# The four sums of weights of each block of a seven-product matrix multiplication: made by GpSimd in a program of its own, in place of VectorE

## The chip, the cores and the metric

One core of one Trainium2 chip runs the whole program once. The metric is the device time of one execution in microseconds (us). The core has five engines that run their own instruction streams and meet only in semaphores: TensorE (matrix products, into eight PSUM banks), VectorE, ScalarE, GpSimd and SyncE (which here only starts the weight transfers).

## The reference, cut to what matters

Two model blocks run one after the other, all in float32, on 256 tokens (272 from the second block on, with 16 meta tokens in front). The change touches three of the four feed-forward layers of the second block, each with a model width of 1024 and a hidden width of 2816:

```python
def swiglu(x, w_in, w_out):
    g, u = jnp.split(x @ w_in, 2, axis=-1)
    return (jax.nn.silu(g) * u) @ w_out

h = h + 0.5 * swiglu(rms_norm(h, ffn_norm[layer]), ffn_w_in[layer], ffn_w_out[layer])
```

## The kernel before, in words

**Weights.** All large weights come from HBM in one long stream of 128 x 128 tiles, 32 tiles (2 MB) to a chunk. For the second block the chunks go to a ring of six slots in SBUF. SyncE starts a transfer when TensorE has moved on from the chunk that held the slot. The ring is filled from the stream without regard to stages, so at the start of a stage the next chunks may already lie in SBUF.

**Stages.** The program is a row of stages. At the end of each, `end_stage` (L831) makes TensorE, ScalarE and VectorE meet, and GpSimd waits for the same semaphore (L854). In the kernel before GpSimd does nothing in a stage except start the small transfers of constants (`load`, L876).

**The paired stages.** Three stages are `swiglu_pairs` (L2592), called "first", "second" and "third paired stage" below: layer 0's second feed-forward layer, layer 1's first, and layer 1's second, which is the last stage of the program. The first two work on 272 tokens in two halves of 136, the third on 256 in two halves of 128. Each has these parts:

- *Plain columns.* The first 2 x 2 output columns of `w_in` are multiplied as usual (32 products with 272 or 256 tokens, from `xg`). They need only x times the norm's gain, which VectorE writes in eight instructions at the very start (`gained`, L2441 to 2444); the division by the root mean square comes later.
- *Paired columns.* The rest is done by a scheme with seven products in place of eight (Winograd's form of Strassen's): two output tiles x two input tiles x two halves of the tokens. It needs sums of the inputs (`add_inputs`, L2556) and sums of the weights (`add_weights`, L2537).
- *Units.* A unit is one pair of output tiles: 4 groups ("columns" in the code) of seven products for `w_in`, 11 for `w_out`. A stage has 20 units for `w_in` and 4 for `w_out`. Two sets of three PSUM banks take turns, so TensorE may start unit n when VectorE has combined unit n - 2 (`combine`, L2570; `banks_free`).
- *Blocks.* A block is as many groups of four weight tiles as fit in what is left of a chunk: 8 groups when it starts on a chunk's border, fewer at the start and the end of a matrix (`pair_blocks`, L127). The blocks of the first paired stage have 2, 8 (nine times), 6 groups for `w_in` and 2, 8 (five times), 2 for `w_out`; of the second 6, 8 (nine times), 2 and 6, 8 (four times), 6; of the third 4, 8 (nine times), 4 and 4, 8 (five times).
- *Sums of weights.* For a block of n groups four instructions of n x 128 elements are issued: s1 = a21 + a22 (L2548), a21 = a11 - a21 in the ring itself (L2550), s2 = s1 - a11 (L2551), s4 = a12 - s2 (L2553). L2550 waits for L2548, L2553 for L2551. The three results s1, s2, s4 lie in one of two buffers; the sums of block b may be written when TensorE has read the last of block b - 2 (`sums_used`). TensorE multiplies the first two products of a block, which need no sums, and then waits for `sums_ready`.

**The order on VectorE** in a paired stage (L2679 to 2724): gained input (eight instructions), root mean square, normed input (L2686, twice), sums of the inputs (four instructions), sums of weights of the blocks that begin in the first 8 groups, plain columns (L2700 to 2705). Then per pair of units: sums of weights, combine, sums of weights, combine, product of gate and up (L2713), four sums of the hidden values (L2558 to 2563). For the units of `w_out`: sums of weights, combine, new x (L2720), in the first two stages squares (L2724). Before each combine `add_weights` makes the sums of those blocks that begin up to 4 groups behind the unit (L2709, L2717). An instruction of VectorE that waits holds up all behind it.

**ScalarE** copies the first product out of PSUM (L2568), makes silu (L2665), and squares or the output transfers.

Of the kernel before, what the change touches and what calls it, by code (L numbers as in the profile page):

```python
# [15 lines left out]
ALU = mybir.AluOpType  # L16
# [8 lines left out]
DT = D // P  # L25
# [219 lines left out]
class Signal:  # L245
# [3 lines left out]
    def __init__(self, sem, count=0):  # L249
        self.sem, self.posts, self.takes, self.turn, self.turn_post = sem, count, count, None, None  # L250
        self.start = count
# [90 lines left out]
def new_signal(K, name):  # L342

    sem, count = K.spare.pop() if K.spare else (K.new_semaphore(name), 0)
    K.counts.append(Signal(sem, count))
    return K.counts[-1]
# [195 lines left out]
def flat(ap):  # L542
    return ap.rearrange("p a t -> p (a t)")
# [1938 lines left out]
class Sevens:  # L2482
# [5 lines left out]
    def __init__(self, K, st, name, half):  # L2488
        sb = lambda n, shape: st.enter_context(K.nc.sbuf_tensor(name + n, shape, F32))
        self.K, self.half = K, half  # L2490
        self.sums, self.head = sb("_weight_sums", [P, 2, 3, KP * P]), sb("_first_product", [P, 2, half])
        self.sums_ready, self.sums_used, self.first_ready, self.head_ready, self.second_ready, self.third_ready, self.banks_free, self.chain = \
            (new_signal(K, name + n) for n in ("_sums", "_sums_used", "_first_bank", "_first_sb", "_second_bank", "_third_bank", "_banks_free",
                                               "_seven_chain"))
        self.combined = self.banks_free.reader()
        self.blocks, self.block_of, self.units, self.columns, self.summed = [], [], [], 0, 0

# [36 lines left out]
            matmul(K, self.part(n, 2, 0), total(2), x("b22", i), i == 0, last, self.sums_used if o == size - 1 else None, shared=True)  # L2534
            matmul(K, self.part(n, 2, 1), tile(3), x("t4", i), False, last, self.third_ready if last else None, shared=True)

    def add_weights(self, dve, upto):  # L2537

        K = self.K
        while self.summed < len(self.blocks) and self.blocks[self.summed][1] < upto:  # L2540
            b = self.summed
            at, _, size = self.blocks[b]
            if b >= 2:
                dve.wait_ge(*self.sums_used.take())
            dve.wait_ge(*K.weights.loaded_at(at))
            a11, a12, a21, a22 = (K.weights.tiles(at + q * size, size) for q in range(4))
            s1, s2, s4 = (self.sums[:, b % 2, q, 0:size * P] for q in range(3))
            dve.tensor_tensor(out=s1, in0=a21, in1=a22, op=ALU.add).then_inc(*self.chain.post())  # L2548
            dve.wait_ge(*self.chain.posted())
            dve.tensor_tensor(out=a21, in0=a11, in1=a21, op=ALU.subtract)  # L2550
            dve.tensor_tensor(out=s2, in0=s1, in1=a11, op=ALU.subtract).then_inc(*self.chain.post())  # L2551
            dve.wait_ge(*self.chain.posted())
            dve.tensor_tensor(out=s4, in0=a12, in1=s2, op=ALU.subtract).then_inc(*self.sums_ready.post())  # L2553
            self.summed += 1

    def add_inputs(self, dve, b11, b12, b21, b22, t1, t2, t4, last):  # L2556
# [35 lines left out]
def swiglu_pairs(K, gain, layer, last=False):  # L2592

    nc, block, bank = K.nc, K.block, K.bank
# [4 lines left out]
    with ExitStack() as st:  # L2599
# [10 lines left out]
        seven = Sevens(K, st, name, half)  # L2610
# [5 lines left out]
        at = K.weights.at + 2 * PLAIN * DT  # L2616
# [13 lines left out]
        @block.tensor  # L2630
        def _(pe):
            for j in range(PLAIN):
                for f in range(2):
                    for k in range(DT):
                        if j == 0 and f == 0:
                            pe.wait_ge(*rms.hn_ready.take())
                        matmul(K, bank[plain_banks[j][f]][:, 0:T], K.weights.take(pe), xg[:, k, :], k == 0, k == DT - 1,
                               gu_ready if k == DT - 1 else None)
            pe.wait_ge(*x_ready.take())
            for n in range(ins):  # L2640
                if n == 1:
                    pe.wait_ge(*plain_free.take(PLAIN))
                seven.tensor(pe, n, inputs)
            for n in range(ins, ins + outs):
                seven.tensor(pe, n, hidden, h_ready if n == ins else None)
            if not last:
                pe.wait_ge(*sq_added.take(2))
                for q in range(2):
                    nc.tensor.matmul(bank[6][:, 0:T], K.con["ones"][:, :], rms.sq[:, q, :], start=q == 0, stop=False)
                pe.wait_ge(*sq_ready.take(outs))  # L2650
                for q in range(2):
                    ins_ = nc.tensor.matmul(bank[6][:, 0:T], K.con["ones"][:, :], squares[:, q, :], start=False, stop=q == 1)
                ins_.then_inc(*rms.summed.post())
            seven.end(pe)

        @block.scalar
        def _(act):
# [9 lines left out]
            for q in range(outs):  # L2667
# [5 lines left out]
                else:  # L2673
                    if q > 1:
                        act.wait_ge(*sq_added.reader().take(q - 1))
                    act.activation((squares if q else rms.sq)[:, :, :], K.x[:, 2 * q:2 * q + 2, :], ACT.Square).then_inc(*sq_ready.post())

        @block.vector
        def _(dve):  # L2679
            chain = seven.chain  # L2680
            rms.gained(dve, gain, layer, xg, t0)
            rms.inverse_root(dve)
            each = rms.rstd[:, t0:T2].rearrange("p (a t) -> p a t", a=1).to_broadcast([P, DT // 2, T])
            dve.wait_ge(*rms.hn_ready.posted())
            for a in (slice(0, DT // 2), slice(DT // 2, DT)):
                dve.tensor_tensor(out=hn[:, a, :], in0=xg[:, a, :], in1=each, op=ALU.mult).then_inc(*chain.post())  # L2686
            dve.wait_ge(*chain.posted())
            a, b = slice(0, DT // 2), slice(DT // 2, DT)
            seven.add_inputs(dve, hn[:, a, lo], hn[:, a, hi], hn[:, b, lo], hn[:, b, hi], hn_sums[:, 0], hn_sums[:, 1], hn_sums[:, 2], x_ready)
            seven.add_weights(dve, DT)  # L2690

            def turn_over(i):
                dve.wait_ge(*h_mult.posted())
                seven.add_inputs(dve, h[:, 2 * i, lo], h[:, 2 * i, hi], h[:, 2 * i + 1, lo], h[:, 2 * i + 1, hi],
                                 h_sums[:, i, 0, :], h_sums[:, i, 1, :], h_sums[:, i, 2, :], h_ready)

            h_mult = chain
            for j in range(PLAIN):
                dve.wait_ge(*gu_ready.take())
                dve.tensor_tensor(out=s[:, j, :], in0=bank[plain_banks[j][0]][:, 0:T], in1=rms.rstd[:, t0:T2], op=ALU.mult).then_inc(*g_scaled.post())  # L2700
                dve.wait_ge(*gu_ready.take())
                dve.tensor_tensor(out=up[:, j, :], in0=bank[plain_banks[j][1]][:, 0:T], in1=rms.rstd[:, t0:T2], op=ALU.mult).then_inc(*plain_free.post())
            dve.wait_ge(*plain_free.posted())
            dve.wait_ge(*s_ready.take(PLAIN))
            dve.tensor_tensor(out=h[:, 0:PLAIN, :], in0=s[:, :, :], in1=up[:, :, :], op=ALU.mult).then_inc(*chain.post())
            turn_over(0)
            for q in range(0, ins, 2):
                for n, o in ((q, gate), (q + 1, other)):
                    seven.add_weights(dve, seven.units[n][0] + seven.units[n][1] + DT // 2)  # L2709
                    seven.combine(dve, n, o[:, :])  # L2710
                i = (PLAIN + q) // 2
                dve.wait_ge(*silu_ready.take())
                dve.tensor_tensor(out=flat(h[:, 2 * i:2 * i + 2, :]), in0=gate[:, 0:2 * T], in1=other[:, 0:2 * T], op=ALU.mult).then_inc(*chain.post())  # L2713
                turn_over(i)
            for q in range(outs):
                n = ins + q
                seven.add_weights(dve, seven.units[n][0] + seven.units[n][1] + DT // 2)  # L2717
                seven.combine(dve, n, other[:, :])
                new = K.x[:, 2 * q:2 * q + 2, t0:T2]
                dve.scalar_tensor_tensor(out=new, in0=other[:, 0:2 * T].rearrange("p (a t) -> p a t", a=2), scalar=0.5, in1=new, op0=ALU.mult, op1=ALU.add)\  # L2720
                   .then_inc(*y_free.post())
                if not last and 0 < q < outs - 1:
                    dve.wait_ge(*sq_ready.reader().take(q + 1))
                    dve.tensor_tensor(out=rms.sq[:, :, :], in0=rms.sq[:, :, :], in1=squares[:, :, :], op=ALU.add).then_inc(*sq_added.post())  # L2724
# [736 lines left out]
def odd_mixer(K):  # L3461
    nc, block, bank, col = K.nc, K.block, K.bank, K.col
    T = T2
    with ExitStack() as st:
# [80 lines left out]
        def _(dve):  # L3545
# [28 lines left out]


STAGES = [rwkv_branch, hgrn_branch, mlstm_branch, lru_branch, merge_and_router, experts, norm_and_swiglu, even_mixer, lambda K: swiglu_pairs(K, "ffn2_norm_2", 0),
          lambda K: swiglu_pairs(K, "ffn1_norm_2", 1), odd_mixer, lambda K: swiglu_pairs(K, "ffn2_norm_2", 1, last=True)]

# [177 lines left out]
```

## Time and profile before

| | us |
|---|---|
| median of 3 runs (2876.89 to 2882.86) | 2877.27 |
| the profiled execution, by its own time | 2879.56 |
| its span from first to last instruction | 2877.8 |
| TensorE busy | 2781.7 (97%) |
| VectorE busy | 1138.8 (40%) |
| ScalarE busy | 375.3 (13%) |
| GpSimd busy | 28.6 (1%) |

The profile is of one execution. Times are counted from its first instruction. A busy TensorE need not be TensorE at its peak, since products are pipelined and their ends are modelled. The trace records each float32 product as two instructions. "PE" is TensorE's products and "PEld" its weight loads, "DVE" VectorE, "ACT" ScalarE, "POOL" GpSimd; a "q" behind the name is the engine's sequencer. The three paired stages lie at about 2092 to 2315, 2315 to 2537 and 2650 to 2878 us. Spans on GpSimd are rough.

### The profile page before, as it was taken

What the parts mean: (1) busy time and instruction counts of PE and PEld (TensorE: products, weight loads), DVE (VectorE), ACT (ScalarE), POOL (GpSimd) and SP (SyncE); (2) the same over time, 40 slices, a digit from 0 to 9 for tenths busy, and PEclk for the clock granted to TensorE, in tenths of its full rate; (3) what the DMA queues carried; (4) which work ended last, traced back from release to release, by engine and by line L of the source; (5) the groups of instructions that cost most, each with busy time, mean ns of one, the idle gap of its engine ahead of it and who ended that gap; (6) DMA issues with size and microseconds to landing.
All of it is one profiled execution on the core that took longest, in us unless ns stands there. A gap on an engine that the chain in (4) does not pass through costs nothing.

```text
span 2877.8 us, 40524 instructions
## 1 busy us (share of the span) xinstructions
PE 2781.7 (97%) x16939; PEld 1907.5 (66%) x16940; DVE 1138.8 (40%) x2357; ACT 375.3 (13%) x772; POOL 28.6 (1%) x56
## 2 busy tenths in 40 slices
PE   8999999989999999999998999999999999998998
PEld 7977778833333333333335888777799999976998
DVE  2644541222222222222223110462377567546674
ACT  1132420200000000000002000122110010012000
POOL 0000000000000000000000000000000000000000
PEclk9999999999999999999999999999999999999999
DMA  5133244469999999999997433332244444432440
GB/s 210 61 105 117 88 145 164 190 240 425 428 429 428 428 429 427 429 428 429 429 427 298 147 146 140 137 117 88 97 147 154 169 145 148 176 142 73 162 147 16
DMA packets 50080, 655.32 MB, mean 228 GB/s; under 512 B 6016, under 2 KB 8208, under 8 KB 10880
## 3 DMA queue, kind: packets, MB, share of 16 engines
q1 hardware_dynamic: 45696, 642.90, 55.7%
q0 software_dynamic: 3104, 9.48, 1.0%
q8 instruction: 103, 1.69, 0.2%
q10 hardware_dynamic: 1152, 1.05, 0.1%
q14 instruction: 25, 0.20, 0.0%
HBM read 652.36 MB, written 1.05 MB: 227 GB/s over the span
## 4 chain that ended last, share of the span: by engine, by line
PE 81%; DMA 9%; DVE 7%; ACT 1%; issue 1%; PEldq 0%; DVEq 0%; SPq 0%; PEld 0%; ACTq 0%
PE bank L357 70%; DMA weight_ring<-weight_stream 8%; PE bank L1163 2%; PE bank L2169 1%; PE bank L2138 1%; DVE expert_hidden L2271 1%; DVE expert_hidden L2270 1%; PE bank L2160 1%; DVE ffn_weight_sums L2553 0%; DVE ffn_weight_sums L2548 0%; DVE weight_ring L2550 0%; ACT expert_y_slots L2216 0%; DVE ffn_weight_sums L2551 0%; DVE mlstm_qk L1536 0%; DMA first_weight_ring<-weight_stream 0%
## 5 line engine op out<-in xcount | busy, mean ns | idle before, releaser
L357 PE MATMUL bank<-weight_ring,expert_x_slots_t 128*64 128x512 f32 x2048 | 459.2, 599 | 3.9 <-DMA weight_ring<-weight_stream 3.9
L357 PEld LDWEIGHTS bank<-weight_ring,expert_x_slots_t 128*64 128x64 f32 x2048 | 141.1, 137 | 319.1 <-issue 305.0
L357 PE MATMUL bank<-x,first_weight_ring 128*128 128x256 f32 x1376 | 316.3, 385 | 16.3 <-DMA first_weight_ring<-weight_stream 8.7
L357 PEld LDWEIGHTS bank<-x,first_weight_ring 128*128 128x128 f32 x1376 | 260.9, 192 | 59.2 <-issue 18.6
L357 PE MATMUL bank<-ffn_x_normed,weight_ring 128*128 128x136 f32 (+1 forms) x1440 | 243.1, 278 | 0.0
L357 PE MATMUL bank<-weight_ring,expert_hidden_slots_t 128*64 128x512 f32 x1024 | 225.2, 592 | 0.0
L357 PE MATMUL bank<-ffn_h,weight_ring 128*128 128x136 f32 (+2 forms) x1144 | 214.6, 313 | 0.5 <-DVE ffn_up L2788 0.5
L357 PEld LDWEIGHTS bank<-ffn_x_normed,weight_ring 128*128 128x128 f32 x1440 | 201.6, 191 | 0.2
L357 PEld LDWEIGHTS bank<-ffn_h,weight_ring 128*128 128x128 f32 x1144 | 177.6, 190 | 14.7 <-DVE ffn_up L2788 1.0
L2280 DVE TENSOR_TENSOR moe_rows<-moe_rows,bank 128x512 f32<-128x512 f32 x128 | 79.4, 683 | 269.0 <-PE bank L2169 269.0
L357 PEld LDWEIGHTS bank<-weight_ring,expert_hidden_slots_t 128*64 128x64 f32 x1024 | 73.4, 137 | 146.4 <-issue 123.3
L357 PE MATMUL bank<-ffn_x_gained,weight_ring 128*128 128x272 f32 x704 | 162.3, 393 | 1.6 <-ACT ffn_x_gained L2371 1.5
L357 PE MATMUL bank<-ffn_x_sums,ffn_weight_sums 128*128 128x136 f32 (+1 forms) x960 | 149.9, 279 | 8.9 <-DVE ffn_weight_sums L2553 8.9
L357 PE MATMUL bank<-even_hn,weight_ring 128*128 128x272 f32 x624 | 154.7, 403 | 0.0
L357 PEld LDWEIGHTS bank<-ffn_x_gained,weight_ring 128*128 128x128 f32 x704 | 133.0, 190 | 30.4 <-ACT ffn_x_gained L2371 3.1
L357 PEld LDWEIGHTS bank<-even_hn,weight_ring 128*128 128x128 f32 x624 | 118.4, 194 | 28.8 <-issue 2.3
L357 PEld LDWEIGHTS bank<-ffn_x_sums,ffn_weight_sums 128*128 128x128 f32 x960 | 128.1, 191 | 10.5 <-DVE ffn_weight_sums L2553 10.5
L2270 DVE TENSOR_SCALAR expert_hidden<-bank 128x512 f32<-128x512 f32 x32 | 22.1, 692 | 196.4 <-PE bank L357 196.4
L357 PE MATMUL bank<-ffn_h_sums,weight_ring 128*128 128x136 f32 (+3 forms) x456 | 97.2, 329 | 2.1 <-DVE ffn_h_sums L2444 2.1
L357 PE MATMUL bank<-ffn_x_sums,weight_ring 128*128 128x136 f32 (+1 forms) x480 | 94.1, 278 | 0.0
L357 PE MATMUL bank<-ffn_x_normed,ffn_weight_sums 128*128 128x136 f32 (+1 forms) x480 | 94.1, 278 | 0.0
L357 PE MATMUL bank<-ffn_h_sums,ffn_weight_sums 128*128 128x136 f32 (+1 forms) x528 | 82.4, 278 | 3.2 <-DVE ffn_weight_sums L2553 3.2
(659 smaller groups left out, 3179.9 us busy)
## 6 DMA issues: line engine op xcount, KB each, us to landing
weight_ring<-weight_stream SPq DMA_DIRECT2D x276, 2048.0 KB, 15.0
first_weight_ring<-weight_stream SPq DMA_DIRECT2D x29, 2048.0 KB, 7.8
first_weight_ring<-weight_stream SPq DMA_DIRECT2D x4, 512.0 KB, 12.1
x<-x_t SPq DMA_DIRECT2D x2, 512.0 KB, 7.0
out_t<-x ACTq DMA_DIRECT2D x8, 128.0 KB, 2.0
c_ret_ret_q<-const_ret_q POOLq DMA_DIRECT2D x1, 544.0 KB, 5.2
c_ret_ret_k<-const_ret_k POOLq DMA_DIRECT2D x1, 544.0 KB, 6.0
c_odd_pool_inv<-const_pool_inv POOLq DMA_DIRECT2D x1, 544.0 KB, 3.8
```

The source lines that it names most:

```text
L357: ins = K.nc.tensor.matmul(out, lhsT, rhs, start=start, stop=stop, skip_group_check=shared)
L1163: ins = nc.tensor.matmul(out(h), lhsT(h), rhs(h), start=start, stop=stop)
L2138: ins = nc.tensor.matmul(bank[3][rows[g], :], pick[:, b, :], K.x_rows[:, b, g * HW:(g + 1) * HW], start=b == 0, stop=b == 1)
L2160: ins = nc.tensor.transpose(bank[5][:, j * P:(j + 1) * P], h[:, 0, j * P:(j + 1) * P], eye)
L2169: ins = nc.tensor.matmul(bank[4 + 2 * b + g][:, :], spread_t[rows[g], b * P:(b + 1) * P], ys[rows[g], :], start=True, stop=True)
L2270: then(dve.tensor_scalar(h[:, 0, :], bank[1][:, :], 7.0, -7.0, ALU.min, ALU.max))
L2271: dve.scalar_tensor_tensor(out=h[:, 0, :], in0=h[:, 0, :], scalar=1.0, in1=gate[:, 0, :], op0=ALU.add, op1=ALU.mult)\
L2280: ins = dve.tensor_tensor(out=part, in0=part, in1=bank[4 + n][:, :], op=ALU.add)
```

## The change

`add_weights` is issued by GpSimd in a program of its own, for all blocks of the stage one after the other, in place of VectorE, where it stood at three places between other work. It waits for what it waited for before (the block's chunk loaded, the sums of block b - 2 used) and no longer for its place in VectorE's order. Its chain of waits has a semaphore of its own. Buffers, blocks and TensorE's program are unchanged.

```diff
-    def add_weights(self, dve, upto):
+    def add_weights(self, pool, upto):
         K = self.K
         while self.summed < len(self.blocks) and self.blocks[self.summed][1] < upto:
...
             if b >= 2:
-                dve.wait_ge(*self.sums_used.take())
-            dve.wait_ge(*K.weights.loaded_at(at))
+                pool.wait_ge(*self.sums_used.take())
+            pool.wait_ge(*K.weights.loaded_at(at))
...
-            dve.tensor_tensor(out=s1, in0=a21, in1=a22, op=ALU.add).then_inc(*self.chain.post())
-            dve.wait_ge(*self.chain.posted())
-            dve.tensor_tensor(out=a21, in0=a11, in1=a21, op=ALU.subtract)
-            dve.tensor_tensor(out=s2, in0=s1, in1=a11, op=ALU.subtract).then_inc(*self.chain.post())
-            dve.wait_ge(*self.chain.posted())
-            dve.tensor_tensor(out=s4, in0=a12, in1=s2, op=ALU.subtract).then_inc(*self.sums_ready.post())
+            pool.tensor_tensor(out=s1, in0=a21, in1=a22, op=ALU.add).then_inc(*self.sum_chain.post())
+            pool.wait_ge(*self.sum_chain.posted())
+            pool.tensor_tensor(out=a21, in0=a11, in1=a21, op=ALU.subtract)
+            pool.tensor_tensor(out=s2, in0=s1, in1=a11, op=ALU.subtract).then_inc(*self.sum_chain.post())
+            pool.wait_ge(*self.sum_chain.posted())
+            pool.tensor_tensor(out=s4, in0=a12, in1=s2, op=ALU.subtract).then_inc(*self.sums_ready.post())
...
+        @block.gpsimd
+        def _(pool):
+            seven.add_weights(pool, seven.columns)
+
         @block.vector
         def _(dve):
...
-            seven.add_weights(dve, DT)
...
-                    seven.add_weights(dve, seven.units[n][0] + seven.units[n][1] + DT // 2)
                     seven.combine(dve, n, o[:, :])
...
-                seven.add_weights(dve, seven.units[n][0] + seven.units[n][1] + DT // 2)
                 seven.combine(dve, n, other[:, :])
```

## Rows read from the trace of the kernel before

**Rows 1.** The page: busy time by engine, with share and instructions.

```profile
PE 2781.7 (97%) x16939; PEld 1907.5 (66%) x16940; DVE 1138.8 (40%) x2357; ACT 375.3 (13%) x772; POOL 28.6 (1%) x56
```

**Rows 2.** TensorE's waits for VectorE's sums: total us, times, longest, by paired stage in order.

```profile
PEld bank L357 <- DVE ffn_weight_sums L2553: 2.6, 2, 1.3
...
PEld bank L357 <- DVE ffn_weight_sums L2553: 0.2, 1, 0.2
...
PEld bank L357 <- DVE ffn_weight_sums L2553: 11.7, 9, 1.3
```

**Rows 3.** The chain that ended last, third paired stage: start us, us, what.

```profile
2693.35 1.23 DVE ffn_weight_sums L2548
...
2697.00 1.24 DVE ffn_weight_sums L2553
...
2698.28 5.19 PE bank L357 x44
...
2705.45 0.70 DVE ffn_h L2713
...
2707.24 1.23 DVE ffn_weight_sums L2548
```

**Rows 4.** The timeline of ScalarE in the third stage's `w_out`: start, us, engine, line.

```profile
2835.03 0.28 ACT L2568 ACTIVATE ffn_first_product<-bank 128x128 f32<-128x128 f32 x1 [16.92 <-PE bank L357]
...
2852.23 0.28 ACT L2568 ACTIVATE ffn_first_product<-bank 128x128 f32<-128x128 f32 x1 [16.92 <-PE bank L357]
```

**Rows 5.** Groups of VectorE instructions by form: xcount | busy us, mean ns | idle before.

```profile
L2550 DVE TENSOR_TENSOR weight_ring<-weight_ring 128x1024 f32<-128x1024 f32 x41 | 50.2, 1225 | 1.4
L2451 DVE RECIPROCAL x_rms<-x_rms 128x272 f32<-128x272 f32 x3 | 5.6, 1854 | 1.5 <-ACT x_rms L2439 1.5
L2550 DVE TENSOR_TENSOR weight_ring<-weight_ring 128x768 f32<-128x768 f32 x4 | 3.8, 958 | 0.1
L2550 DVE TENSOR_TENSOR weight_ring<-weight_ring 128x512 f32<-128x512 f32 x3 | 2.1, 692 | 0.1
L2550 DVE TENSOR_TENSOR weight_ring<-weight_ring 128x256 f32<-128x256 f32 x4 | 1.7, 426 | 0.1
```

**Rows 6.** The chain again, where the first stage goes from `w_in` to `w_out`.

```profile
2236.57 1.24 DVE ffn_weight_sums L2548
...
2240.22 1.24 DVE ffn_weight_sums L2553
...
2241.50 1.54 PE bank L357 x11
```

**Rows 7.** Windows around the second stage's start; behind the engines' busy times: PEclk, DMA, GB/s.

```profile
2313.00:2315.00 2.00, 1.18 (x4) 0.68 (x4) 0.18 (x1) 0.54 (x2) 0.00 (x0) 0.96 0.82 352
2315.00:2317.00 2.00, 1.76 (x4) 1.41 (x5) 2.00 (x9) 1.04 (x1) 0.00 (x0) 0.50 0.00 0
2317.00:2319.00 2.00, 2.00 (x7) 1.53 (x7) 1.50 (x3) 1.52 (x2) 0.00 (x0) 0.69 0.00 0
2319.00:2321.00 2.00, 2.00 (x11) 1.65 (x10) 1.97 (x2) 0.20 (x1) 0.00 (x0) 1.00 0.00 0
```

**Rows 8.** The timeline of the first stage's start, VectorE and TensorE.

```profile
2091.68 2.26 DVE L2444 TENSOR_SCALAR ffn_h_sums<-x,columns_sb 128x272 f32<-128x272 f32 x8 [1.53 <-PEq L839]
...
2092.10 14.94 PE L357 MATMUL bank<-ffn_h_sums,weight_ring 128*128 128x272 f32 x64 [0.70 <-DVE ffn_h_sums L2444]
...
2096.68 2.49 DVE L2686 TENSOR_TENSOR ffn_x_normed<-ffn_h_sums,x_rms 128x1088 f32<-128x1088 f32 x2
...
2101.36 0.72 DVE L2563 TENSOR_TENSOR ffn_x_sums<-ffn_x_normed,ffn_x_sums 128x544 f32<-128x544 f32 x1
...
2106.87 0.63 PE L357 MATMUL bank<-ffn_x_normed,weight_ring 128*128 128x136 f32 x4
```

**Rows 9.** The timeline of GpSimd and VectorE at the start of another stage.

```profile
2537.97 0.54 POOL L880 DMA_DIRECT2D c_odd_pool_inv<-const_pool_inv  x1
...
2538.40 1.71 DVE L2468 TENSOR_SCALAR odd_y<-x,columns_sb 128x272 f32<-128x272 f32 x6
2538.50 0.64 POOL L880 DMA_DIRECT2D c_odd_pair_gather<-const_pair_gather  x1
...
2540.22 0.54 POOL L880 DMA_DIRECT2D odd_sinks<-in_od_sinks  x1
```

More of the change, by code:

```diff
@@ L2491, in __init__ @@
         self.sums, self.head = sb("_weight_sums", [P, 2, 3, KP * P]), sb("_first_product", [P, 2, half])
-        self.sums_ready, self.sums_used, self.first_ready, self.head_ready, self.second_ready, self.third_ready, self.banks_free, self.chain = \
+        self.sums_ready, self.sums_used, self.first_ready, self.head_ready, self.second_ready, self.third_ready, self.banks_free, self.chain, self.sum_chain = \
             (new_signal(K, name + n) for n in ("_sums", "_sums_used", "_first_bank", "_first_sb", "_second_bank", "_third_bank", "_banks_free",
-                                               "_seven_chain"))
+                                               "_seven_chain", "_sum_chain"))
         self.combined = self.banks_free.reader()
```

## The prediction

> **What bounds the kernel now.** I read the busy line of the page first: TensorE works 97% of the span, VectorE 40%, GpSimd 1% [rows 1]. So only what makes TensorE idle counts, and of that only what VectorE's sums of weights cause. TensorE's waits name them [rows 2]: 2.6 us in the first paired stage (2 waits), 0.2 in the second (1), 11.7 in the third (9). About 14.5 us of 2878 is all that the sums hold up today.
>
> The chain shows how the third stage loses its share [rows 3]. VectorE ends the hidden product and its sums, only then starts the sums of the next block at 2693.35, and TensorE goes on at 2698.28; the next turn begins at 2707.24. A turn of one block of 8 groups (56 products) takes 13.89 us. In the same stage 77 products without a wait take 2852.23 - 2835.03 = 17.20 us [rows 4], so 56 take 12.51. Each turn loses 1.38 us.
>
> **The change, part by part.** The sum is made against the profiled execution, 2879.56 us; the median of the runs is 2.3 us below it, and I move the median by the same difference.
>
> *Removed: VectorE's place in the order.* Of the third stage's nine waits eight are such turns: 8 x 1.38 = 11.0 us. The ninth stands where `w_in` meets `w_out`. Of the first stage's two waits one is of this kind (1.3), the other is at its junction. Gone: 12.3 us, if GpSimd can make a block's sums while TensorE works on one block. VectorE loses some 208 instructions (4 x 52 blocks), about 4.9 us of every 13; it was not the bound, so that alone gives nothing more.
>
> *Price of a sum on GpSimd.* No row shows GpSimd doing arithmetic. The nearest rows are VectorE's: 1.225 us for the same instruction, and at the far end its slowest elementwise one, 1.854 us for 272 elements, which would be 7.0 us for 1024 [rows 5]. The operation is the plain one, so it stands nearer to the first; since both operands must be read I take twice that row: 2.45 us, 9.8 for a block of 8, and by the smaller forms 7.7 for 6 groups, 5.5 for 4, 3.4 for 2. That is below 12.5 to 13.0 us of TensorE per block, so in the steady part the sums are hidden. They stop being so beyond 3.2 us per instruction.
>
> The Trainium skill (GPSIMD Engine Reference, section 3.1) gives 4497 ns for 2048 float32 elements on GpSimd and 2293 on VectorE. From that I estimate 2.28 us for 1024. By that price the junctions below would cost 2 us less. No run here shows it yet; VectorE's 1.225 us agrees with it.
>
> *Added: the junctions.* The sums of block b start when block b - 2 is used up, that is when TensorE starts b - 1. If b - 1 is small and b large, nothing covers them. In the first stage block b - 1 has 2 groups: 14 products and the two that need no sums last 3.7 us (16 products of 136 tokens, at between 17.20/77 = 0.223 us, the third stage's with 128 tokens, and 136/128 of that, 0.237). VectorE needed 4.93 us (2236.57 to 2241.50 [rows 6]) and TensorE idled 1.2 to 1.3. GpSimd at 9.8 leaves 6.1. In the second stage 6 groups follow 2: 7.7 - 3.7 = 4.0, against 0.2 today. In the third 8 groups follow 4: 9.8 - 6.7 = 3.1, against 1.2. Added: 13.2 - 2.7 = 10.5 us.
>
> *Clock.* An idle TensorE can lose clock: after the pauses at the end of the first stage its granted clock stood at 0.50, the level of 1.2 GHz, for 2 us and at 0.69 for 2 more [rows 7]. That is 2 x 0.5 + 2 x 0.31 = 1.6 us lost. I count one such loss, at the 6 us pause; bounds 0 and 4.8.
>
> So far: -12.3 + 10.5 + 1.6 = -0.2 us. The large expected gain is eaten by three junctions.
>
> *Moved: the sums of the first two blocks to the stage's very start.* Before, VectorE made them after the inputs, under the plain products. GpSimd starts them with the stage, since b below 2 waits for nothing but the chunk, and the ring is full (no transfer runs in 2315 to 2321 [rows 7]). In just these microseconds VectorE has its only work that TensorE waits for at once: eight gained inputs in 2.26 us, the first of which lets TensorE start 0.4 us later; products last 14.94/32 = 0.467 us, so the eighth input is wanted about 3.7 us into the stage [rows 8]. Whether an instruction of VectorE is delayed by one of GpSimd that reads the same memory, no row shows. The lower bound is no delay. The upper bound is turn by turn: each input behind the first waits out one GpSimd instruction. I take a middle: GpSimd pauses twice in a block for its own chain, and VectorE gets two through in each pause, so that the eight wait out the four sums of block 0 and one of block 1. First stage (2 groups): 3.4 + 2.45 + 2.2 of its own = 8.1, wanted at 3.7: +4.4. Second (6): 7.7 + 2.45 + 2.2 = 12.3: +8.6. Third (4): 5.5 + 2.45 + 2.1 = 10.1, wanted at 3.5: +6.6. Together +20 us. Turn by turn with three large sums in place of one adds 4.9 to each: +34. Behind them, normed inputs and their sums end at 2102.1 where TensorE wants them at 2106.9 [rows 8]; that slack of 4.8 us moves along with TensorE, and I count nothing for it (bounds 0 and 3.6).
>
> The only hint in the trace: a transfer that GpSimd issued just after six such VectorE instructions began took 0.64 us, its neighbours 0.54 [rows 9]. VectorE's own six are as quick as elsewhere. Weak, but not nothing.
>
> The Trainium skill (SBUF — State Buffer, Who interferes with whom) says that a VectorE instruction with two SBUF inputs, or one in a two-port mode, and a GpSimd instruction that reads SBUF exclude each other for a whole instruction. By that rule the delay at the stage starts is real and speaks against this change. No row before shows the two side by side, so the rule is untested here.
>
> *Elsewhere* the two meet in L2713 and the sums behind it (2.0 us per pair of units). Turn by turn they would last at most about 10 us; VectorE has some 9 to 11 us until TensorE wants the next banks, and where the first stage's blocks begin they hardly overlap. Cost nothing; if that cover is gone it becomes the bound below. Queues: GpSimd's stage constants are issued after a stage and its sums before its end, so nothing stands behind them; SyncE's transfers follow TensorE as before.
>
> **Sum:** 2879.6 - 0.2 + 20 = 2899.4 for a profiled execution, 2897 for the median.
>
> **The rivals.** *The engines don't disturb each other* (not slower): everything above but the stage starts, 2877, within 2 us. For it: VectorE's durations in [rows 9]. It decides as soon as the gained inputs keep their 2.26 us.
>
> *The sums are cheap on GpSimd* (faster): at VectorE's own price the junctions stay as they are and 12.3 us go: 2865. The gain passes 0.2% (5.8 us) below about 2.1 us per instruction with undisturbed stage starts. Against it: nothing in the trace but the pure guess of equal speed.
>
> *GpSimd becomes the bound* (slower): above 3.2 us per instruction each of some 38 large blocks waits. At three times VectorE, 14.8 us per block, 26 blocks lose 1.8 and 12 lose 2.3 us, minus 12.3 removed, plus larger junctions (15) and the start: about 2940 to 2960.
>
> *It doesn't do what it says*: first use of GpSimd for arithmetic might cost a one-off, hidden under 15 us of plain products; 2877.
>
> **How the numbers follow.** A measurement of this kernel can tell about 0.2%, 5.8 us, from no change. Disturbed starts: 0.50, 2887 to 2914 as its own range. Undisturbed: 0.27, of which 0.19 the same, 0.04 faster, 0.04 slower. Cheap sums: 0.10, faster. GpSimd bound: 0.09, slower. Nothing but a one-off: 0.04, same. Faster 0.14, same 0.23, slower 0.63. The range from 2868 to 2920 takes in turn by turn with a clock loss and most of the cheap case; left out are the GpSimd bound, the last of the cheap case and the sum of all upper bounds.
>
> **What would show each step.** GpSimd: 2.45 us mean for 1024 elements, 52 x 4 instructions. The third stage: turns of 12.5 us and no wait of TensorE at eight blocks. Three waits of TensorE for GpSimd's L2553, of 6, 4 and 3 us. L2444 spread over 8, 12 and 10 us with GpSimd's sums between. The prediction is wrong if L2444 keeps its 2.26 us, or if TensorE waits at every block.

## The result and the profile after

The changed kernel takes 2920.64 us (median of 4 runs, 2916.77 to 2923.7) against 2877.3 before: 43 us slower, ratio 1.0145 with a 95% interval of 1.0133 to 1.0158. The forecast was 2897 with a range of 2868 to 2920. The direction and the kind of mechanism were right; the forecast change, 20 us, was less than half of what came. The ratios of the experiments below are to runs of the kernel before made beside each of them, with medians of 2879.4 to 2881.4 us, so differences between absolute times from different sessions are good to some 4 us.

Busy time by engine on the page of the changed kernel, with share and instructions (before: [rows 1]):

```profile
PE 2807.1 (96%) x16939; PEld 1920.3 (66%) x16940; DVE 1033.8 (35%) x2149; ACT 374.7 (13%) x772; POOL 478.2 (16%) x264
```

VectorE lost 208 instructions, GpSimd gained 208. What the sums cost there, by form (xcount | busy us, mean ns | idle before), beside [rows 5]:

```profile
L2550 POOL TENSOR_TENSOR weight_ring<-weight_ring 128x1024 f32<-128x1024 f32 x41 | 97.8, 2386 | 3.2
L2550 POOL TENSOR_TENSOR weight_ring<-weight_ring 128x768 f32<-128x768 f32 x4 | 7.2, 1812 | 0.3
L2550 POOL TENSOR_TENSOR weight_ring<-weight_ring 128x512 f32<-128x512 f32 x3 | 3.8, 1271 | 0.2
L2550 POOL TENSOR_TENSOR weight_ring<-weight_ring 128x256 f32<-128x256 f32 x4 | 2.9, 728 | 0.3
```

The guess of twice VectorE (2.45 us) was close: 2.39 us, four of them well under the 12.5 to 13.0 us of a block. GpSimd is not the bound. TensorE's waits for other engines' results in the three paired stages in order (total us, times, longest), beside [rows 2]:

```profile
PEld bank L357 <- DVE ffn_h_sums L2444: 9.1, 8, 2.1
PEld bank L357 <- POOL ffn_weight_sums L2553: 6.5, 1, 6.5
...
PEld bank L357 <- DVE ffn_h_sums L2444: 14.4, 8, 2.8
PEld bank L357 <- POOL ffn_weight_sums L2553: 4.1, 1, 4.1
...
PEld bank L357 <- DVE ffn_h_sums L2444: 12.6, 8, 2.2
PEld bank L357 <- POOL ffn_weight_sums L2553: 3.5, 1, 3.5
```

The nine waits of the third stage became one. The three of GpSimd are the junctions. Those for L2444, the gained inputs, now come eight times in each stage, once for every input. The timeline of VectorE and GpSimd at the second stage's start shows how (the lines between are left out; beside [rows 8]):

```profile
2333.03 1.98 DVE L2444 TENSOR_SCALAR ffn_h_sums<-x,columns_sb 128x272 f32<-128x272 f32 x1 [2.22 <-PEq L839]
...
2333.05 1.80 POOL L2548 TENSOR_TENSOR ffn_weight_sums<-weight_ring 128x768 f32<-128x768 f32 x1 [16.70 <-PEq L839]
...
2338.63 1.96 DVE L2444 TENSOR_SCALAR ffn_h_sums<-x,columns_sb 128x272 f32<-128x272 f32 x1
2338.63 1.80 POOL L2553 TENSOR_TENSOR ffn_weight_sums<-weight_ring,ffn_weight_sums 128x768 f32<-128x768 f32 x1
...
2340.39 2.40 POOL L2548 TENSOR_TENSOR ffn_weight_sums<-weight_ring 128x1024 f32<-128x1024 f32 x1
...
2340.51 2.44 DVE L2444 TENSOR_SCALAR ffn_h_sums<-x,columns_sb 128x272 f32<-128x272 f32 x1
...
2342.87 2.49 DVE L2444 TENSOR_SCALAR ffn_h_sums<-x,columns_sb 128x272 f32<-128x272 f32 x1
...
2342.87 2.34 POOL L2550 TENSOR_TENSOR weight_ring<-weight_ring 128x1024 f32<-128x1024 f32 x1
```

One gained input, 0.36 us by itself, ends with each GpSimd instruction. In the first stage the first input still took its 0.36 us and seven waited; in the second and third all eight waited, the first for 1.98 and 1.42 us. The eight together, in the three stages:

```profile
2094.81 10.60 DVE L2444 TENSOR_SCALAR ffn_h_sums<-x,columns_sb 128x272 f32<-128x272 f32 x8 [1.53 <-PEq L839]
...
2333.03 17.11 DVE L2444 TENSOR_SCALAR ffn_h_sums<-x,columns_sb 128x272 f32<-128x272 f32 x8 [2.22 <-PEq L839]
...
2686.75 14.92 DVE L2444 TENSOR_SCALAR ffn_h_sums<-x,columns_sb 128x256 f32<-128x256 f32 x8 [1.53 <-PEq L839]
```

Before they took 2.26, 2.26 and 2.19 us. The pauses also cost TensorE its clock. Windows of the second stage's start in the changed kernel (after the busy times: PEclk, DMA, GB/s; before: [rows 7]) and of the junctions of the first, second and third stage:

```profile
2333.00:2337.00 4.00, 1.33 (x3) 0.56 (x3) 3.97 (x3) 1.25 (x1) 3.87 (x3) 0.76 0.00 0
2337.00:2341.00 4.00, 2.85 (x5) 1.30 (x6) 4.00 (x3) 0.00 (x0) 3.92 (x3) 0.50 0.00 0
...
2349.00:2353.00 4.00, 2.86 (x7) 2.19 (x7) 3.47 (x4) 1.71 (x2) 0.99 (x1) 0.50 0.00 0
2353.00:2357.00 4.00, 4.00 (x13) 3.10 (x12) 3.93 (x5) 0.00 (x0) 0.00 (x0) 0.68 0.00 0
...
2256.00:2259.50 3.50, 0.49 (x2) 0.50 (x3) 3.07 (x3) 0.00 (x0) 3.42 (x3) 0.58 0.96 412
2259.50:2263.00 3.50, 3.50 (x17) 3.50 (x17) 0.00 (x0) 0.00 (x0) 3.42 (x2) 0.50 0.00 0
...
2500.00:2504.00 4.00, 4.00 (x26) 4.00 (x26) 3.65 (x3) 0.00 (x0) 3.92 (x3) 0.71 0.00 0
...
2850.00:2854.00 4.00, 3.52 (x17) 3.52 (x18) 0.57 (x1) 0.00 (x0) 3.92 (x3) 0.57 0.00 0
```

At 0.50 TensorE runs at 1.2 of its 2.4 GHz. In the second stage the clock had fallen at this place before too, for some 3 us; now, with one product every 1.8 to 2.5 us, it stays down for 20. At the first junction TensorE works again from 2259.0 and stands at 0.50 until 2263.4: 2.2 us lost. At the other two the clock falls just behind the restart: the second reads 0.72 in the 2 us from 2498 and 0.71 in the 4 us from 2500, 1.7 us lost together, and the third 0.57, again 1.7. In the kernel before no clock was lost at a junction.

**Where 44 us of the profiled execution came from.** The three paired stages grew by 15.1, 20.2 and 7.0 us (from the first L2444 of a stage to the first VectorE instruction of the stage behind it, or to the end), together 42.3.

| | us |
|---|---|
| starts: to the first paired product a stage takes 24.3, 31.4 and 28.5, before 15.2, 16.7 and 14.3 (clock included) | +38.0 |
| waits at the junctions: 14.1, before 2.7 | +11.4 |
| clock at the junctions | +5.6 |
| waits gone | -12.3 |
| sum | 42.7 |

The sum also holds stage by stage, to 0.2 us. The rest of the 44 us lies outside the three stages: 3.1 us ahead of the first, where the two kernels are the same, and 1.3 us the other way between the second and the third.

### The profile page after: what moved, and what is told of

It reads as the page before. It is cut to its first block, busy times and chain, and to the rows that moved or that the text cites. A ratio compares the mean times of both kernels' runs of the same rounds, so it can differ in the third digit from the quotient of the medians.

```text
span 2921.9 us, 40538 instructions
## 1 busy us (share of the span) xinstructions
PE 2807.1 (96%) x16939; PEld 1920.3 (66%) x16940; DVE 1033.8 (35%) x2149; ACT 374.7 (13%) x772; POOL 478.2 (16%) x264
## 4 chain that ended last, share of the span: by engine, by line
PE 84%; DMA 8%; DVE 5%; ACT 1%; POOL 1%; issue 1%; PEldq 0%; DVEq 0%; PEld 0%; SPq 0%; ACTq 0%; POOLq 0%
PE bank L357 72%; DMA weight_ring<-weight_stream 7%; PE bank L1163 2%; PE bank L2169 1%; DVE ffn_h_sums L2444 1%; PE bank L2138 1%; DVE expert_hidden L2271 1%; DVE expert_hidden L2270 1%; PE bank L2160 1%; ACT expert_y_slots L2216 0%; PE bank L3343 0%; PE bank L2875 0%; PE bank L3322 0%; PE bank L725 0%; PE bank L3190 0%
## 5 line engine op out<-in xcount | busy, mean ns | idle before, releaser
L357 PEld LDWEIGHTS bank<-ffn_h,weight_ring 128*128 128x128 f32 x1144 | 179.9, 193 | 14.7 <-DVE ffn_up L2789 1.0
L2548 POOL TENSOR_TENSOR ffn_weight_sums<-weight_ring 128x1024 f32<-128x1024 f32 (+3 forms) x52 | 111.9, 2152 | 399.3 <-PEq L839 200.6
L357 PE MATMUL bank<-ffn_h_sums,weight_ring 128*128 128x136 f32 (+3 forms) x456 | 116.6, 368 | 21.5 <-DVE ffn_h_sums L2444 21.2
L2577 DVE TENSOR_TENSOR ffn_up_pair<-bank,ffn_first_product 128x272 f32<-128x272 f32 (+1 forms) x42 | 18.3, 436 | 301.7 <-ACT ffn_first_product L2568 301.7
L2551 POOL TENSOR_TENSOR ffn_weight_sums<-ffn_weight_sums,weight_ring 128x1024 f32<-128x1024 f32 (+3 forms) x52 | 116.8, 2247 | 0.0
## 6 DMA issues: line engine op xcount, KB each, us to landing
weight_ring<-weight_stream SPq DMA_DIRECT2D x276, 2048.0 KB, 14.7
```

The lines of the kernel that those rows point to most:

```text
L357: ins = K.nc.tensor.matmul(out, lhsT, rhs, start=start, stop=stop, skip_group_check=shared)
L2548: pool.tensor_tensor(out=s1, in0=a21, in1=a22, op=ALU.add).then_inc(*self.sum_chain.post())
L2551: pool.tensor_tensor(out=s2, in0=s1, in1=a11, op=ALU.subtract).then_inc(*self.sum_chain.post())
L2577: dve.tensor_tensor(out=o.rearrange("p (b a t) -> p b a t", b=2, a=4)[:, :, 0, :], in0=two(self.part(n, 0, 1, 2)), in1=twice(self.head[:, ...
```

## The experiments

**First: is it the stage's start?** Two theories of the disturbance stood against each other and against a third, that the junctions cost everything.

*GpSimd waits for the gained inputs.*

```diff
+        gained_at = rms.hn_ready.sem, rms.hn_ready.posts + DT
+
         @block.gpsimd
         def _(pool):
+            pool.wait_ge(*gained_at)
             seven.add_weights(pool, seven.columns)
```

> The changed kernel, but GpSimd begins its sums only when VectorE has written all eight gained inputs. Theory T (a VectorE instruction that reads two SBUF tensors, or the gained input's kind, and a GpSimd sum exclude each other, turn by turn): L2444 is back at 2.3 us, and the disturbance moves to the normed inputs and their sums (six instructions with two SBUF inputs), which end some 20 us into the stage instead of 10.4, where TensorE wants them at 15: about 5 us per stage, 2893 us in all. Rival A (only the gained inputs are disturbed): 2878 to 2880 us. Rival B (the stage start has nothing to do with it, the junctions and the clock cost the 43 us): 2915 to 2920 us.

Measured: 2905.68 us, ratio to the kernel before 1.0089 (1.0072 to 1.0106). L2444 is back at 2.26 us, and the disturbance moves on to the instructions with two SBUF inputs. The timelines of VectorE and GpSimd in the first stage:

```profile
2090.64 2.26 DVE L2444 TENSOR_SCALAR ffn_h_sums<-x,columns_sb 128x272 f32<-128x272 f32 x8 [1.53 <-PEq L839]
...
2093.75 1.85 DVE L2451 RECIPROCAL x_rms<-x_rms 128x272 f32<-128x272 f32 x1 [0.50 <-ACT x_rms L2439]
2095.64 4.87 DVE L2693 TENSOR_TENSOR ffn_x_normed<-ffn_h_sums,x_rms 128x1088 f32<-128x1088 f32 x2
2100.55 2.76 DVE L2558 TENSOR_TENSOR ffn_x_sums<-ffn_x_normed 128x544 f32<-128x544 f32 x1
...
2095.97 3.40 POOL L2548 TENSOR_TENSOR ffn_weight_sums<-weight_ring 128x1024 f32<-128x1024 f32 x1
2099.45 3.28 POOL L2550 TENSOR_TENSOR weight_ring<-weight_ring 128x1024 f32<-128x1024 f32 x1
2102.68 2.83 POOL L2551 TENSOR_TENSOR ffn_weight_sums<-ffn_weight_sums,weight_ring 128x1024 f32<-128x1024 f32 x1
```

L2558 took 0.72 us before; L2693 (before L2686) 2.49. The delay goes both ways here: GpSimd's sums of 1024 elements, 2.35 us by themselves, took up to 3.40. TensorE waited 4.1, 5.7 and 6.4 us for the inputs' sums. The reciprocal, with one SBUF input, ran beside GpSimd's sums and kept its 1.85 us. So theory T holds: both kinds of instruction wait, and rivals A and B are out. But the total is 13 us above the forecast. The waits explain 16 us, as expected; the forecast had nothing for the junctions (some 5 us more than what was removed), and nothing for the clock behind these new waits, which read 0.52 and 0.62 in the two windows of 4 us from 2108.

*VectorE makes the first two blocks' sums at the old place*, GpSimd the rest. Each engine waits for the other's `sums_ready` where it takes over.

```diff
+    def by_vector(self, b):
+        return b < 2
...
+            if b and self.by_vector(b) != self.by_vector(b - 1):
+                pool.wait_ge(self.sums_ready.sem, self.sums_ready.start + b)
...
             seven.add_inputs(dve, ..., x_ready)
+            seven.vector_weights(dve, DT)
...
```

> VectorE makes the sums of the first two blocks of a stage at their old place, GpSimd all others. Theory T and rival A: the stage starts cost nothing, what is left is the junctions (waits of 6.5, 4.1 and 3.5 us, one or two clock losses of 1.6 us) minus 12.3 us removed: 2877 to 2881 us. Rival B: 2915 to 2920 us.

Measured: 2886.55 us (10 runs, 2879.55 to 2894.53), ratio 1.0026 (1.0014 to 1.0038). That takes back 34 of the 43 us, so the stage starts are the largest part of the loss; rival B is out again. It is 5.6 us above the upper end of the forecast. Left over are the junctions with their clock and one new wait, in TensorE's waits in the first stage:

```profile
PEld bank L357 <- POOL ffn_weight_sums L2572: 6.5, 1, 6.5
PEld bank L357 <- DVE ffn_gate_pair L2603: 2.2, 1, 2.2
```

There the first hidden sums (L2558 and on, L2576 and on in this run) fell into GpSimd's third block, took 2.3 to 2.5 us each in place of 0.3, and pushed the combine behind them past the time when TensorE wanted its banks.

**Second: what kind of instruction waits?**

*ScalarE writes the gained inputs*, GpSimd starts with the stage.

```diff
         @block.scalar
         def _(act):
+            for j in range(DT):
+                act.activation(xg[:, j, :], K.x[:, j, t0:T2], ACT.Identity, scale=K.col(gain, layer * DT + j)).then_inc(*rms.hn_ready.post())
             rms.scalar(act)
...
-            rms.gained(dve, gain, layer, xg, t0)
...
-            dve.wait_ge(*rms.hn_ready.posted())
+            dve.wait_ge(*gained_at)
```

> GpSimd makes all sums from the stage's start as in the changed kernel, but ScalarE writes the eight gained inputs (8 x 0.43 us). Theory T: ScalarE is not disturbed, TensorE starts at once; the normed inputs on VectorE take turns with the sums and end at 18 to 22 us where 15 are allowed: 2888 to 2894 us. Rival A: 2878 to 2882 us. Rival C (a GpSimd sum slows whoever writes or reads SBUF next to it, also ScalarE): L2444's work on ScalarE spreads over 8 to 15 us, 2915 us.

Measured: 2900.91 us, ratio 1.0078 (1.0061 to 1.0095). The eight ran on ScalarE beside GpSimd's sums at 0.43 us each, the time of its squares of the same size (L2416), so ScalarE is not disturbed and rival C falls:

```profile
2088.70 3.41 ACT L2661 ACTIVATE ffn_h_sums<-x,columns_sb 128x272 f32<-128x272 f32 x8 [1.02 <-PEq L839]
```

VectorE's two-input instructions were disturbed: TensorE waited 2.3, 6.0 and 4.7 us for L2563. The total is 7 us above the forecast, which had left out the same two things, the junctions and the clock.

*The gained inputs in odd pieces.*

```diff
+        odd = (T2 - t0) // 2 + 1
...
-            dve.tensor_scalar(xg[:, j, :], self.K.x[:, j, t0:T2], ...).then_inc(*self.hn_ready.post())
+            dve.tensor_scalar(xg[:, j, 0:odd], self.K.x[:, j, t0:t0 + odd], ...)
+            ins = dve.tensor_scalar(xg[:, j, odd:T2 - t0], self.K.x[:, j, t0 + odd:T2], ...)
+            ins.then_inc(*self.hn_ready.post())
```

> The changed kernel, but each gained input is written in two VectorE instructions of an odd number of elements (137 and 135, in the last stage 129 and 127), one SBUF input each. [...] Rival C' (any VectorE instruction takes turns with a sum): sixteen turns, 20 us or more before the last input, 2930 us or more.

Measured: 2927.68 us, ratio 1.0164 (1.0147 to 1.0181). Odd pieces wait too, but not each of them:

```profile
2099.87 0.28 DVE L2445 TENSOR_SCALAR ffn_h_sums<-x,columns_sb 128x137 f32<-128x137 f32 x1
2100.07 2.36 DVE L2446 TENSOR_SCALAR ffn_h_sums<-x,columns_sb 128x135 f32<-128x135 f32 x1
2102.35 2.38 DVE L2445 TENSOR_SCALAR ffn_h_sums<-x,columns_sb 128x137 f32<-128x137 f32 x1
2104.65 0.28 DVE L2446 TENSOR_SCALAR ffn_h_sums<-x,columns_sb 128x135 f32<-128x135 f32 x1
```

Between two sums one or two short pieces get through. The run had been expected at 2888 to 2896 us, in the belief that a one-input instruction with an odd number of elements stays out of the two-port mode and does not collide with GpSimd. It is 32 us above that. The belief was a misreading: the Trainium skill (VectorE: DVE Perf Modes, What auto-detection actually checks) asks for outermost sizes that are both even or equal, and input and output of a piece are equal. So oddness does not rule the two-port mode out, and this run doesn't test it. The durations say that the pieces did not leave the gained input's own mode: undisturbed, 135 or 137 elements took 0.28 us and 272 took 0.36, some 0.6 ns more for each further element, where a two-input `tensor_tensor` goes from 0.30 (136 elements) to 0.44 us (272), 1.0 ns for each. Whole or in odd pieces, the gained input runs at about twice the rate of a two-input instruction, which fits the two-port mode and doesn't prove it. Whether a one-input `tensor_scalar` that is surely outside that mode would run undisturbed wasn't tried; the reciprocal above is the only sign of it.

**Third: turn by turn, or a share of the time?**

*Short sums.* GpSimd makes the sums of the first two blocks in pieces of 256 elements.

```diff
+            piece = 2 * P if b < 2 else size * P
+
+            def pieces(out, in0, in1, op):
+                for c in range(0, size * P, piece):
+                    ins = pool.tensor_tensor(out=out[:, c:c + piece], in0=in0[:, c:c + piece], in1=in1[:, c:c + piece], op=op)
+                return ins
+
+            pieces(s1, a21, a22, ALU.add).then_inc(*self.sum_chain.post())
...
```

> The changed kernel, but GpSimd makes the sums of the first two blocks of a stage in pieces of 256 elements (0.73 us each) in place of instructions of up to 1024 (2.36 us); same arithmetic, and more GpSimd time in all. Theory T (turn by turn: each gained input waits out one GpSimd instruction, however long): the eight take about 8 x (0.73 + 0.2) = 7 to 8 us in every stage in place of 10.6, 17.1 and 14.9, which is some 20 us less in all: 2895 to 2905 us. Rival S (the engines share in proportion to their load): L2444 spreads as before or longer, 2920 us or more.

Measured: 2887.75 us, ratio 1.002 (1.0011 to 1.003), 33 us below the changed kernel, with more work on GpSimd than there. VectorE's eight inputs in the three stages:

```profile
2088.74 5.67 DVE L2444 TENSOR_SCALAR ffn_h_sums<-x,columns_sb 128x272 f32<-128x272 f32 x8 [1.53 <-PEq L839]
...
2320.04 6.14 DVE L2444 TENSOR_SCALAR ffn_h_sums<-x,columns_sb 128x272 f32<-128x272 f32 x8 [2.22 <-PEq L839]
...
2656.56 6.18 DVE L2444 TENSOR_SCALAR ffn_h_sums<-x,columns_sb 128x256 f32<-128x256 f32 x8 [1.54 <-PEq L839]
```

About 6 us in every stage, seven or eight turns of 0.7 to 0.8 us. The price of a stage's start is the length of the seven or eight GpSimd instructions that run beside the inputs, not the time that GpSimd works, so rival S is out. It came out 7 us better than the forecast, since these 6 us keep TensorE nearly fed (waits of 1.1 to 1.7 us at most): to the first paired product the three stages now take 17.3, 17.8 and 17.1 us, 6 us more than before in place of 38.

**Fourth: the junctions.**

*The block behind the small one on VectorE too.*

```diff
     def by_vector(self, b):
-        return b < 2
+        return b < 2 or self.blocks[b - 1][2] < 6 and self.blocks[b][2] > self.blocks[b - 1][2]
```

> VectorE makes the sums of the first two blocks and of the block behind the small one in the middle (block 12 in the first and third paired stage, 11 in the second), GpSimd all others. Theory J (a junction costs GpSimd's extra time over a small block, 14.1 us of waits, plus TensorE's clock after them): the three waits go back to 1.2, 0.2 and 1.2 us, and the total falls by 11 us and 2 to 3 us of clock below the run with only the first two blocks on VectorE (2886.6): 2872 to 2876 us. Rival K (VectorE's sums of hidden values, held up by GpSimd, take the time elsewhere, and the junction's wait only hides it): less than 4 us gained, 2882 us or more.

Measured: 2869.96 us, ratio to the kernel before 0.9964 (0.9951 to 0.9978): faster than before. That is 2 us below the forecast. Waits at the junctions are 1.3, 0.2 and 1.3 us. Theory J holds: 16.6 us for 11.3 us of waits, so the clock's part is some 5 us, where the windows of the changed kernel gave 5.6 and the forecast 2 to 3.

*A third buffer.* Over the run with the first two blocks on VectorE, the small block in the middle keeps its sums in the idle buffers of silu, up and the squares, and the wait is for the block that last used the same buffer.

```diff
-            if b >= 2:
-                pool.wait_ge(self.sums_used.sem, self.sums_used.start + b - 1)
+            if self.place(b)[1] is not None:
+                pool.wait_ge(self.sums_used.sem, self.sums_used.start + self.place(b)[1] + 1)
...
```

> The first two blocks on VectorE, all others on GpSimd, and the small block in the middle has a third buffer for its sums (in the idle buffer of silu and up), so that GpSimd may start the block behind it one block earlier. Theory J: no wait for the sums at a junction is left, 14.1 us and 2 to 3 us of clock below 2886.6: 2868 to 2872 us, faster than the kernel before. Rival K: 2880 us or more.

Measured: 2871.85 us, ratio 0.9974 (0.9963 to 0.9986), as forecast. No wait for sums is left in any paired stage; the 2.2 us for L2603 (now L2618) in the first stage are still there.

*The third buffer alone, all sums on GpSimd*: the same edit of the buffers, on the changed kernel.

> The changed kernel with the third buffer for the small block in the middle and nothing else. Theory J: 14.1 us of waits and 2 to 3 us of clock below the changed kernel's 2920.6: 2902 to 2905 us; L2444 still spread over 11, 17 and 15 us. Rival (the junctions were hidden behind something else): above 2912 us.

Measured: 2906.08 us, ratio 1.0091 (1.0076 to 1.0107): 14.6 us below the changed kernel, with L2444's waits unchanged at 9.1, 14.4 and 12.6 us. It is 1 us above the forecast. What is left is the cost of the stage starts, less the waits that the change removed.

**Last: was another engine needed?** The kernel before, GpSimd idle, with the sums in the third stage made one unit earlier.

```diff
-                    seven.add_weights(dve, seven.units[n][0] + seven.units[n][1] + DT // 2)
+                    seven.add_weights(dve, seven.units[n][0] + seven.units[n][1] + (DT if last else DT // 2))
```

> GpSimd is not used at all: the kernel before, where in the third paired stage VectorE makes the sums of a block one unit earlier, in front of the combine of the second unit of a pair, where it idled 4.1 us. Theory L (the 11 to 12 us of waits in the third stage come from VectorE's order, not from its load): the nine waits go, 2867 to 2869 us, as fast as the best split with GpSimd. Rival M (VectorE is too loaded, the sums only push the combine back): no gain, 2877 to 2881 us.

Measured: 2870.08 us, ratio 0.996 (0.9948 to 0.9972), 1 us above the forecast and as fast as the best split with GpSimd. The timeline of VectorE in the third stage, first in the kernel before, where this combine stood behind 4.2 us of idle time, then in this run:

```profile
2689.99 0.42 DVE L2577 TENSOR_TENSOR ffn_up_pair<-bank,ffn_first_product 128x256 f32<-128x256 f32 x1 [4.20 <-ACT ffn_first_product L2568]
...
2701.59 1.23 DVE L2548 TENSOR_TENSOR ffn_weight_sums<-weight_ring 128x1024 f32<-128x1024 f32 x1
...
2705.25 1.23 DVE L2553 TENSOR_TENSOR ffn_weight_sums<-weight_ring,ffn_weight_sums 128x1024 f32<-128x1024 f32 x1
2706.39 0.41 DVE L2577 TENSOR_TENSOR ffn_up_pair<-bank,ffn_first_product 128x256 f32<-128x256 f32 x1
```

No wait of TensorE for sums is left in this stage. The third stage's waits, 11.0 of the 12.3 us that the change removed, came from VectorE's order, not from its load.

## Why the prediction was wrong

Its steps one by one.

- *Removed, 12.3 us:* right. The third stage's eight turns lost their wait, and the one wait of this kind in the first stage went. The last experiment shows for the third stage that VectorE's place in the order was the cause.
- *Price of a sum, 2.45 us:* right, 2.39 measured, 1.81, 1.27 and 0.73 for the smaller forms where 1.92, 1.38 and 0.85 stood. The Trainium skill's price (GPSIMD Engine Reference, section 3.1), 2.28 by my estimate, is close too; an undisturbed sum took 2.35 to 2.36.
- *Junctions:* right, waits of 6.5, 4.1 and 3.5 us where 6.1, 4.0 and 3.1 stood; 16.6 us with their clock were won back by moving three blocks.
- *Clock:* too low. I counted one loss of 1.6 us, and each of the three junctions had one, 5.6 us together; the upper bound was 4.8. The clock lost at the stage starts was in no term.
- *The stage starts:* this is the step that failed. "VectorE gets two through in each pause": it gets one through for each GpSimd instruction, also at GpSimd's own waits, so the eight inputs wait out seven sums in the first stage and eight in the others, not five. They took 10.6, 17.1 and 14.9 us where the text had 8.1, 12.3 and 10.1. I had +4.4, +8.6 and +6.6 us, +20 in all; measured to the first paired product +9.1, +14.7 and +14.2, +38.0. By the prediction's own measure, the time by which the eighth input is late, it is +6.9, +13.4 and +11.4, or 31.7, near the +34 of turn by turn; some 6 us more went to TensorE's lower clock. Turn by turn would have forecast 2911. Both ends were in the text and the middle had no row behind it.
- *Elsewhere:* nearly right. The hidden product and its sums did take turns (L2713, now L2715, 0.69 to 2.43 us in the third stage; L2558 0.30 to 1.93 in the second), covered as forecast. The run with the first two blocks on VectorE shows that the cover is thin: one such meeting cost TensorE 2.2 us.
- *Rivals:* "the engines don't disturb each other" fell at once. GpSimd as the bound never came.

The rule of the Trainium skill that I cited against the change (SBUF — State Buffer, Who interferes with whom) is borne out: two-input instructions took 2.76 us in place of 0.72, and the gained inputs up to 2.50 in place of 0.36. ScalarE took 3.41 us for the eight inputs, undelayed. That the gained inputs belong to its two-port kind fits their rate but is left open.

The range missed by less than 1 us on its bad side, but not because I left out a sum of upper ends. With the upper bounds of the starts (34) and of the clock (4.8) together my terms give 2914, inside the range. The terms themselves were short: 38.0 against that 34, 5.6 of clock against 4.8 and 11.4 at the junctions against 10.5 make the other 6 us. The starts and the clock have the same cause, a starved TensorE, and grow together; I bounded them as if they were independent.

## What to carry to other kernels

Before moving work to an engine whose instructions make another's wait, list what that other does with one urgent result after the next at the same moment. Here each of those waited out one whole instruction of the newcomer, so its length, not its load, set the price. Shorter pieces took back 33 us of the 43. A start a few microseconds later took back only 15, since the next instructions waited instead. And read the chain first: when the bound engine waits for an engine that idles a few microseconds earlier in the same turn, the order can be mended without any other engine.

## What the runs showed that I had not expected

The turns are strict even where GpSimd waits on its own semaphore between two sums: one gained input of 0.36 us per sum, seven or eight times in a row. Pieces of half the length got through in twos at times. The first arithmetic of the program on GpSimd had no one-off cost: 0.85 us for 256 elements beside VectorE's inputs, and 0.73, the same as later, where ScalarE wrote them. And the pauses of 3.5 to 6.5 us, in which TensorE had nothing, cost 1.7 to 2.2 us more in clock after they ended.
